# First output projection of a two-block layer in seven products instead of eight

## The chip, the cores and the metric

The kernel runs on one core of a Trainium2 chip. The metric is device time in microseconds; the kernel before takes 2780.12 us (median of 3 runs, 2779.41 to 2782.68). The engines are named as in the profile: PE (TensorE) multiplies, ACT (ScalarE) and DVE (VectorE) do the elementwise work, POOL (GpSimd) a little of it and some transfers, SP only issues transfers. Each engine runs its own list of instructions in order; they meet at semaphores alone.

## The reference, cut to what matters

Two blocks follow each other, both in float32, on 512 tokens with width 2048. What the change touches is the end of the first block:

```python
# first block: y_a, y_b are [512, 2048] each
y_a = _rmsnorm(y * silu(z_ssd), g_ssd)
y_b = _rmsnorm(u * sg * silu(z_mlp), g_mlp)
mix = concatenate([y_a, y_b], axis=-1) @ w_out     # [512, 4096] @ [4096, 2048]
x = x + gate * _rmsnorm(mix, g_post)
# second block begins with h = rms_norm(x, norm_gain) * (1 + scale) + shift
```

A row factor of the norm (one number for each token) comes out of the product, so the kernel multiplies by it when it takes results out of PSUM: `ra` for the first 2048 columns of the concatenation, `rb` for the second.

## The kernel before, in words

**Precision.** Every float32 matrix is split into a high part (a copy rounded to fp32r, made by ACT) and a low part (the rest, made by DVE), and a product is three matmuls: high by high, high by low, low by high. A weight unit is 128 partitions by 1024 numbers, 512 KB. SP loads it into one of three buffers `RAW`, ACT makes `WH`, DVE makes `WL` (four buffers each), PE uses both. ACT and DVE make units two ahead of PE (`make(u + 2)`), SP loads four ahead (`raw_load(u + 4)`); a buffer `RAW` is free when `hi` and `lo` of its unit are made, `WH` and `WL` when PE has `used` the unit.

**The projection** (`o_unit`, line 535, and the loop around it) has 64 units, 192 to 255 (`AT_OUT` is 192). A unit holds 2 tiles of 128 rows by 512 columns of `w_out`. For each of 4 token blocks `k` and both tiles it gives three matmuls of 128x512: 24 matmuls a unit, 1536 in all. The outer loops are `half` (which part of the concatenation) and `nb` (which 512 output columns); the four token blocks stand in four PSUM banks, and two sets of four banks alternate. The inputs come from `SY` in DRAM, in 32 loads by POOL (`y_load`); ACT and DVE scale and split each one (`turn_half`). Results of half 0 are scaled into `O` by ACT, those of half 1 are added by DVE. The last four units are used in the order of token blocks, so that one block of `O` after another is complete while PE goes on.

**The tail.** For each token block `k`: squares of its four column blocks (ACT, `jk`), their sum (DVE), a factor (POOL, `first_factor`), the product with the gain `gg` (DVE, `gain_out`), the new x in two halves (DVE, `make_x1`), its squares (ACT, `XR<-O`), a second factor (POOL, `second_factor`), the scaled rows (`XR`, ACT and DVE), and then PE transposes them (`turn_row`, L838). The first matmul of the second block (L437 after 1797 us) needs transposed tiles of all four token blocks.

**Work that lies beside it.** The last gates of the first block (16 in number) are spread over PE's list: `gate(g)` is a generator on each engine, stepped between units. For gate g, SP loads `vg`, `wsg` and `bsg`, DVE makes `wsr` from `wsg` (four small operations), PE multiplies (L755), DVE makes `sgt` and goes on to `GA`. Gate 14 follows PE's first unit of the projection, gate 15 its third. SP may load gate g+1 only when DVE has made `sgt` of gate g.

## Time and profile before

| what | value |
|---|---|
| median of the runs | 2780.12 us |
| profiled execution, span from first to last instruction | 2778.7 us |
| PE busy | 2740.8 us, 99% |
| DVE, ACT, POOL busy | 1471.3, 1061.1, 339.1 us |
| TensorE clock granted, mean over the span | 0.998 of full speed |
| first matmul of the projection / last one / first of the second block | 1432.72 / 1783.88 / 1797.25 us |

The profile gives the profiled execution's time as its span, 2778.7 us; the median of the runs is 1.4 us more, for what lies before the first and after the last instruction. Starts are counted from the span's start. A matmul of 128x512 is listed with some 0.39 us because neighbours overlap in the array; what counts is the distance of their starts. A line can be that of a helper: L1031 is every operation of ACT, L1650, L1654 and L1658 are helpers of DVE, L2501 is every load of SP. The tile names tell them apart.

### The profile page before, as it was taken

How to read it: one execution, taken by the hardware profiler on the slowest of the kernel's cores; microseconds unless marked ns; L12 is line 12 of the kernel's file. 1: busy time of each engine (PE TensorE's matmuls, PEld its weight loads, DVE VectorE, ACT ScalarE, POOL GpSimd, SP SyncE). 2: the span in 40 equal slices, each digit the busy share in tenths (PEclk: the TensorE clock that was granted, in tenths of full speed). 3: DMA queues.
4: the chain of work that ended last, by engine and by line, in shares of the span. 5: the costliest groups of instructions: out<-in, count | busy, mean ns of one | idle time of the engine just before them, and what ended most of it. 6: DMA issues, size and time to landing. Idle time of an engine off the chain costs nothing. (4 is left out here: it accounts for less than half of the span.)

```text
span 2778.7 us, 33018 instructions
## 1 busy us (share of the span) xinstructions
PE 2740.8 (99%) x13142; PEld 2231.2 (80%) x13142; DVE 1471.3 (53%) x1794; ACT 1061.1 (38%) x1420; POOL 339.1 (12%) x417
## 2 busy tenths in 40 slices
PE   6999999999999999999999999899999999999999
PEld 3688888888888888888888888788888888788787
DVE  2377767765565456766652332634445443533733
ACT  3332222334333333433332332535556553442611
POOL 2101000102233323331310000100000000000000
PEclk9999999999999999999999999999999999999999
DMA  9667766744545464555454433332222223223252
GB/s 399 254 234 260 274 233 251 278 159 154 179 146 169 156 185 151 160 169 175 150 190 180 134 113 99 119 102 83 84 83 89 78 83 103 87 91 99 102 179 91
DMA packets 162120, 439.34 MB, mean 158 GB/s; under 512 B 14768, under 2 KB 59824, under 8 KB 151728
## 3 DMA queue, kind: packets, MB, share of 16 engines
q1 hardware_dynamic: 122208, 303.08, 32.7%
q0 software_dynamic: 16944, 97.18, 9.9%
q10 hardware_dynamic: 22816, 36.97, 3.8%
q8 instruction: 105, 1.72, 0.3%
q14 instruction: 47, 0.39, 0.0%
HBM read 398.11 MB, written 39.06 MB: 157 GB/s over the span
## 5 line engine op out<-in xcount | busy, mean ns | idle before, releaser
L1650 DVE TENSOR_TENSOR WL<-RAW,WH 128x1024 fp32r<-128x1024 f32 (+1 forms) x424 | 519.0, 1232 | 744.9 <-ACT WH L1031 568.9
L437 PE MATMUL PB<-HH,WH 128*128 128x512 f32 x2048 | 818.6, 400 | 2.4 <-DVE WL L1650 2.4
L442 PE MATMUL PB<-HL,WH 128*128 128x512 f32 x2048 | 801.6, 391 | 0.0
L443 PE MATMUL PB<-HH,WL 128*128 128x512 f32 x2048 | 801.3, 391 | 0.0
L1031 ACT ACTIVATE WH<-RAW 128x1024 fp32r<-128x1024 f32 (+1 forms) x424 | 433.4, 1038 | 444.0 <-PE PB L549 252.6
L547 PE MATMUL PB<-WH,HH 128*128 128x512 f32 x1248 | 490.0, 393 | 1.6 <-ACT Kr L1031 0.8
L549 PE MATMUL PB<-WH,HL 128*128 128x512 f32 x1248 | 486.1, 390 | 0.0
L548 PE MATMUL PB<-WL,HH 128*128 128x512 f32 x1248 | 485.9, 389 | 0.0
L437 PEld LDWEIGHTS PB<-HH,WH 128*128 128x128 f32 x2048 | 385.0, 188 | 103.3 <-issue 22.6
L442 PEld LDWEIGHTS PB<-HL,WH 128*128 128x128 f32 x2048 | 385.6, 188 | 65.6 <-issue 3.1
L443 PEld LDWEIGHTS PB<-HH,WL 128*128 128x128 f32 x2048 | 385.0, 188 | 66.2
L547 PEld LDWEIGHTS PB<-WH,HH 128*128 128x128 f32 x1248 | 234.4, 188 | 51.5 <-issue 2.5
L549 PEld LDWEIGHTS PB<-WH,HL 128*128 128x128 f32 x1248 | 234.3, 188 | 49.3
L548 PEld LDWEIGHTS PB<-WL,HH 128*128 128x128 f32 x1248 | 234.4, 188 | 49.0 <-issue 1.0
L1658 DVE SCALAR_TENSOR_TENSOR AACC<-AU,small,AACC 128x2048 f32<-128x2048 f32 x60 | 140.9, 2349 | 68.1 <-DMA AU<-in_w_ada 68.0
L441 PE MATMUL PB<-CL,WH 128*128 128x256 f32 x384 | 108.3, 282 | 0.0
L440 PE MATMUL PB<-CH,WH 128*128 128x256 f32 x384 | 107.7, 281 | 0.0
L2409 POOL TENSOR_TENSOR xw<-xk,wk 128x256 f32<-128x256 f32 x80 | 75.1, 964 | 262.9 <-ACT xk L1031 161.9
L445 PE MATMUL PB<-CH,WL 128*128 128x256 f32 x384 | 106.8, 278 | 0.0
L1031 ACT ACT_TABLE_LOAD x77 | 98.8, 1283 | 6.3 <-DVE wk L1650 3.5
L1658 DVE SCALAR_TENSOR_TENSOR ca<-zp,par,ca 128x512 f32<-128x512 f32 x128 | 95.4, 746 | 7.9 <-ACT ca L1031 6.9
L1031 ACT ACTIVATE zp<-PB 128x512 f32<-128x512 f32 x32 | 18.9, 603 | 188.3 <-PE PB L445 171.4
(326 smaller groups left out, 2534.4 us busy)
## 6 DMA issues: line engine op xcount, KB each, us to landing
RAW<-in_w_in_t SPq DMA_DIRECT2D x312, 512.0 KB, 3.6
AU<-in_w_ada POOLq DMA_DIRECT2D x64, 1024.0 KB, 5.5
RAW<-in_w_out_t SPq DMA_DIRECT2D x96, 512.0 KB, 3.6
bcb<-R SPq DMA_DIRECT2D x64, 256.0 KB, 6.1
S<-so ACTq DMA_DIRECT2D x24, 384.0 KB, 2.5
ebc<-R SPq DMA_DIRECT2D x32, 256.0 KB, 6.0
SY<-evb ACTq DMA_DIRECT2D x32, 256.0 KB, 2.9
yin<-SY POOLq DMA_DIRECT2D x32, 256.0 KB, 4.0
```

The lines of the kernel that those rows point to most:

```text
L437: h.matmul(banks[j], lh, m.HH[:, t, :], start=st, stop=False)
L440: h.matmul(cb, lh, m.CH[:, t, :], start=st and j == 0, stop=False, skip_group_check=True)
L441: h.matmul(cb, lh, m.CL[:, t, :], start=False, stop=False, skip_group_check=True)
L442: h.matmul(banks[j], lh, m.HL[:, t, :], start=False, stop=False)
L443: ins = h.matmul(banks[j], ll, m.HH[:, t, :], start=False, stop=en)
L445: ins = h.matmul(cb, ll, m.CH[:, t, :], start=False, stop=en, skip_group_check=True)
L547: h.matmul(bank, xh, wh[:, tt, :], start=t == 0, stop=False)
L548: h.matmul(bank, xh, wl[:, tt, :], start=False, stop=False)
L549: ins = h.matmul(bank, xl, wh[:, tt, :], start=False, stop=t == 15)
L1031: return h.activation(o, a, f, **kw)
L1650: return h.tensor_tensor(o, a, b, op)
L1658: return h.scalar_tensor_tensor(out=o, in0=a, scalar=sc, in1=b, op0=op0, op1=op1)
```

## The change

The projection is done by a form of Strassen's multiplication. It runs in 8 groups `q`; the chunk `c = q // 2` is a fourth of the 4096 rows of `w_out`, and `n = q % 2` a half of the output columns. In a group a 2 by 2 block product (tokens in halves, rows in halves, columns in halves of 512) takes 7 products `ph` instead of 8, each of 2 weight units (`ab`) and 24 matmuls of 128x512. The number of units goes from 64 to 112.

- **Left side.** The chunk of y is loaded by SP (`load_y`) into `F`, scaled in place by ACT (`scale_tile`), POOL makes four sums (`sum_S`, 128x1024 each), and each of the 7 forms is split into `FH` (ACT) and `FL` (DVE). Forms are made once for two groups.
- **Right side.** SP loads B11, B21 and B22 of a group. The four sums E, F, H and G are made in the tile: POOL issues a DMA that adds a block of `w_out` to what the buffer holds (`accum_op=ADD`). E, F and G follow each other in one pair of buffers, each added when DVE has made `lo` of the one before; H is added to B22's pair. Each such step is two DMAs of 512 KB.
- **PSUM.** Three pairs of banks, X, Y and Z, in the order Y, X, Z, Z, Y, Y, Y. A product that stays in its pair adds to what is there, and PE waits until the bank's content has been taken out. Taking out is `evacuate`: in the first two groups mostly ACT, after that DVE alone, 14 operations a group.
- **Squares and gains.** ACT squares finished blocks of `O` in group 7; 12 of the 16 products with the gain `gg` go from DVE to POOL, the other four stay on DVE. Token blocks 0 and 1 have their last part in products 1 and 4 of group 7, blocks 2 and 3 in products 5 and 6, the last two. `XR` and `gg` are loaded by SP instead of POOL.

```diff
-UNITS_IN, UNITS_OUT, UNITS_IN2, UNITS_OUT2 = 192, 64, 128, 32
+UNITS_IN, UNITS_OUT, UNITS_IN2, UNITS_OUT2 = 192, 112, 128, 32
...
+def form_unit(q, ph, ab):
+
+    return AT_OUT + 14 * q + 2 * ph + ab
...
+def pair_of(q, ph):
+
+    return (q % 2, 3, q % 2, 2, q % 2, 2, q % 2)[ph]
...
+def out_source(q, row, col, ab):
+    c, n = divmod(q, 2)
+    return (2 * n + col) * 16 + 4 * c + 2 * row + ab
+
+
+def forms_due(q, ph):
+    c = q // 2
+    if q == 0:
+        return {0: [(0, 3)], 1: [(0, 4)], 3: [(0, 5)], 4: [(0, 6)]}.get(ph, [])
+    if q % 2:
+        return [(c + 1, f) for f in {1: [0], 2: [1], 4: [2], 6: [3]}.get(ph, [])] if c < 3 else []
+    return [(c, f) for f in {0: [4], 1: [5], 2: [6]}.get(ph, [])]
+
+
+def tiles_due(q, ph):
+    c = q // 2
+    if c < 3 and q % 2 == 0 and ph == 6:
+        return [(c + 1, i) for i in range(4)]
+    if c < 3 and q % 2 and ph == 0:
+        return [(c + 1, i) for i in range(4, 8)]
+    return []
...
+    X, Y, Z = ([ring.popleft() for j in range(2)] for ring in (main, main, hb))
+    m.bank.update({(nm, j): b[j] for nm, b in (("X", X), ("Y", Y), ("Z", Z)) for j in range(2)})
+
+    def bank_ready(q, ph, j):
+        if q == 0 and ph < 3:
+            reuse((Y, X, Z)[ph][j])
+        elif ph < 3:
+            P.wait_ge(*at("ev", q - 1, (6, 1, 3)[ph], j))
+        else:
+            P.wait_ge(*at("ev", q, (2, 0, 4, 5)[ph - 3], j))
+
+    def product(q, ph):
+        for j in range(2):
+            bank = PB[(Y, X, Z, Z, Y, Y, Y)[ph][j]]
+            bank_ready(q, ph, j)
+            P.wait_ge(*at("fl", q // 2, ph))
+            for ab in range(2):
+                n = form_unit(q, ph, ab)
+                split_ready(n)
+                wh = m.WH[n % 4].rearrange("p (t c) -> p t c", t=2)
+                wl = m.WL[n % 4].rearrange("p (t c) -> p t c", t=2)
+                for tt in range(2):
+                    p = 2 * ab + tt
+                    xh, xl = m.FH[ph][:, p, j * 128:(j + 1) * 128], m.FL[ph][:, p, j * 128:(j + 1) * 128]
+                    h.matmul(bank, xh, wh[:, tt, :], start=p == 0 and ph < 3, stop=False,
+                             skip_group_check=True)
+                    h.matmul(bank, xh, wl[:, tt, :], start=False, stop=False, skip_group_check=True)
+                    ins = h.matmul(bank, xl, wh[:, tt, :], start=False, stop=p == 3, skip_group_check=True)
+                if j:
+                    ins.then_inc(*put(s.unit, "used", n))
+                elif ab:
+                    ins.then_inc(*put(s.block, "half", q, ph))
+            if q == 0:
+                step(bg2)
+
+    for q in range(GROUPS):
+        for ph in range(7):
+            product(q, ph)
+            if q == 0 and ph == 5:
+                drain(bg2)
+                b, bank = take(hb, "gate sums")
+                P.wait_ge(*at("GA", 15))
+                column_sums(b, bank, m.GA, "gate sums")
+                drop(hb, b, ("rb sum",))
...
+    def form_high(c, f):
+        if f in (0, 1, 6):
+            A.wait_ge(*at("y scaled", c, 3 if f == 0 else 7))
+            A.wait_ge(*at("S", c, {2: 1, 4: 2, 5: 3, 3: 4}[f]))
...
+        if c:
+            A.wait_ge(*at(*form_free(c, f)))
+        else:
+            A.wait_ge(*at("ra sum"))
+            A.wait_ge(*at("YA", 7, 1))
+        A.then(act(m.FH[f], m.form[f], ACT.Copy), "fh", c, f)
...
+        if (q, ph) in ((0, 0), (0, 2), (0, 4), (0, 6), (1, 0), (1, 2), (1, 3), (1, 6)):
+            return
+        c, n = divmod(q, 2)
+        k = j if ph in (0, 1, 3, 4) else 2 + j
+        col = 1024 * n + (0 if ph in (0, 1, 6) else 512)
+        dst = add = m.O[:, k, col:col + 512]
+        V.wait_ge(*at(*out_done(q, ph, j)))
+        V.wait_ge(*at("ran" if c < 2 else "rbn"))
+        if (q, ph) == (0, 1):
+            add = m.t1[j]
+            V.wait_ge(*at("sg", 15))
+            V.wait_ge(*at("sgt", 15))
+            V.wait_ge(*at("ev", 0, 0, j))
+        elif (q, ph) == (0, 3):
+            add = m.t2[j]
+            V.wait_ge(*at("gate sums"))
+            V.wait_ge(*at("ev", 0, 4, j))
+        elif ph in (1, 4, 5):
+            V.wait_ge(*at("ev", q, (0, 3, 2)[(1, 4, 5).index(ph)], j))
+        else:
+            V.wait_ge(*at("ev", q - 2, {0: 1, 3: 3 if q == 2 else 4, 2: 5, 6: 6}[ph], j))
+        r = (m.ran, m.rbn) if ph in (4, 5) else (m.ra, m.rb)
+        V.then(STT(dst, bank("YXZZYYY"[ph], j), r[c // 2][:, k:k + 1], add, ALU.mult, ALU.add), "ev", q, ph, j)
...
+    def add_load(q, ph, before, row, col, ab, *key):
+        i = pair_of(q, ph)
+        G.wait_ge(*at("lo", form_unit(q, before, ab)))
+        h.dma_start(m.WP[i][ab], I["w_out_t"][out_source(q, row, col, ab)], accum_op=ALU.add) \
+            .then_inc(*land(s.wsum[2 * i + ab], *key, q, ab))
...
+    sum_S(0, 1)
+    sum_E(0)
+    for i in 2, 3, 4:
+        sum_S(0, i)
+    for q in range(GROUPS):
+        sum_F(q)
+        sum_H(q)
+        sum_G(q)
+        if q % 2 and q < 7:
+            for i in 1, 2, 3, 4:
+                sum_S(q // 2 + 1, i)
+        if q < 7:
+            sum_E(q + 1)
...
+    for k in range(4):
+        gain(k, 0)
+        gain(k, 1)
+    gain(0, 2)
+    gain(1, 2)
     first_factor(0)
+    first_factor(1)
+    gain(2, 3)
+    gain(3, 3)
+    first_factor(2)
     second_factor(0)
-    first_factor(1)
+    first_factor(3)
     second_factor(1)
-    first_factor(2)
-    first_factor(3)
     second_factor(2)
     second_factor(3)
...
+    def load_B21(q, ab):
+        if q:
+            Y.wait_ge(*at("lo", form_unit(q - 1, 1, ab)))
+        else:
+            Y.wait_ge(*(at("used", AT_OUT - 2) if ab else at("lo", AT_OUT - 1)))
+        out_load(q, 1, 1, 0, ab, "B21")
...
     drain(bg)
-    for u in range(AT_OUT, AT_IN2):
-        raw_load(u + 4)
-        step(bg2, 2)
+    load_B21(1, 0)
+    load_B21(1, 1)
+    drain(bg2)
```

SP's list around the loads for gates 14 and 15 (`vg`, `wsg`, `bsg`; `RAW` are weight buffers). Before:

```order
436 L2501 DMA RAW_53<-in_w_out_t 128x1024 [waits lo,hi]
437 L2501 DMA RAW_54<-in_w_out_t 128x1024 [waits lo,hi]
438 L2501 DMA vg<-VT 128x512 [waits VT2,dve_side,pe_side]
439 L2501 DMA wsg<-in_w_s_t 128x128
440 L2501 DMA bsg<-in_bs 128x128
441 L2501 DMA RAW_55<-in_w_out_t 128x1024 [waits lo,hi]
442 L2501 DMA RAW_53<-in_w_out_t 128x1024 [waits lo,hi]
443 L2501 DMA vg<-VT 128x512 [waits VT3,dve_side,pe_side]
```

The same place now (`hold` are further weight buffers; rows 443 and 444 are `load_B21(1, 0)` and `load_B21(1, 1)`):

```order
442 L2683 DMA hold_190<-in_w_out_t 128x1024
443 L2683 DMA RAW_55<-in_w_out_t 128x1024 [waits lo]
444 L2683 DMA hold_191<-in_w_out_t 128x1024 [waits lo]
445 L2683 DMA vg<-VT 128x512 [waits VT2,dve_side,pe_side]
446 L2683 DMA wsg<-in_w_s_t 128x128
447 L2683 DMA bsg<-in_bs 128x128
448 L2683 DMA vg<-VT 128x512 [waits VT3,dve_side,pe_side]
```

The load for gate 14 stood behind the weight load of unit 196, whose buffer is free after `lo` and `hi` of unit 193; it now stands behind two loads that wait for `lo` of units 194 and 195.

DVE's list at the same place now (`wsr` is gate 14's; `WL2_62` and `WL3_63` are the low parts of units 194 and 195, `FL3_177` that of a form, the last two those of the sum E):

```order
941 L1758 TENSOR_TENSOR WL2_62<-RAW2_55,WH2_58 128x1024 [waits unit,hi,wp6]
942 L1758 TENSOR_TENSOR WL3_63<-hold4_191,WH3_59 128x1024 [waits unit,hi,wp7]
943 L1762 TENSOR_SCALAR wsr_139<-wsg_137,small_66 128x128 [waits wsg]
944 L1762 TENSOR_SCALAR wsr_139<-wsg_137,small_66 128x128 x3
945 L1758 TENSOR_TENSOR FL3_177<-E0_185,FH3_176 128x1024 [waits act_side]
946 L1758 TENSOR_TENSOR WL0_60<-RAW0_53,WH0_56 128x1024 [waits unit,hi,wsum0]
947 L1758 TENSOR_TENSOR WL1_61<-RAW1_54,WH1_57 128x1024 [waits unit,hi,wsum1]
```

`wsr` stands behind the low part of unit 195, and the E sums behind `wsr`.

POOL's list at the end of the projection now; before, it held only the eight factors there (each a TENSOR_SCALAR and a TENSOR_TENSOR on `small`):

```order
439 L2574 DMA hold_189<-in_w_out_t 128x1024 [waits lo]
440 L2574 DMA hold_190<-in_w_out_t 128x1024 [waits lo]
441 L2569 TENSOR_TENSOR O<-O,gg 128x512 [waits act_side,gg]
442 L2569 TENSOR_TENSOR O<-O,gg 128x512 [waits act_side] x9
443 L2446 TENSOR_SCALAR small<-small 128x1 [waits dve_side]
444 L2443 TENSOR_TENSOR small<-small,cst 128x1 [waits pool_side]
445 L2446 TENSOR_SCALAR small<-small 128x1 [waits dve_side]
446 L2443 TENSOR_TENSOR small<-small,cst 128x1 [waits pool_side]
447 L2569 TENSOR_TENSOR O<-O,gg 128x512 [waits act_side] x2
```

Ten products with the gain now stand between the last adding DMA and the first factor.

## Rows read from the trace of the kernel before

**Rows 1.** The page's first part: busy time, share, instructions of each engine.
```profile
PE 2740.8 (99%) x13142; PEld 2231.2 (80%) x13142; DVE 1471.3 (53%) x1794; ACT 1061.1 (38%) x1420; POOL 339.1 (12%) x417
```

**Rows 2.** Busy time by window; last columns clock, DMA share, GB/s.
```profile
1640.00:1760.00 120.00, 120.00 (x531) 99.41 (x530) 42.64 (x46) 31.36 (x46) 0.00 (x0) 1.00 0.30 97
1780.00:1800.00 20.00, 11.95 (x52) 9.63 (x51) 16.04 (x26) 16.17 (x26) 6.88 (x10) 0.74 0.37 147
```

**Rows 3.** PE's timeline where the projection begins: start, us, instruction [idle before].
```profile
1432.72 0.39 PE L547 MATMUL PB<-WH,HH 128*128 128x512 f32 x1
...
1438.52 1.13 PE L755 MATMUL PB<-wsr,vg 128*128 128x128 f32 x8 [0.20 <-DVE wsr L1654]
```

**Rows 4.** PE's timeline at its end and after it.
```profile
1783.88 0.40 PE L829 MATMUL PB<-WH,HL 128*128 128x512 f32 x1
1792.69 0.90 PE L838 MATMUL PB<-cst,XR 128*128 128x128 f32 x3 [7.76 <-ACT XR L1031]
1793.78 3.83 PE L838 MATMUL PB<-cst,XR 128*128 128x128 f32 x15 [0.18 <-DVE XR L1654]
1797.25 0.78 PE L437 MATMUL PB<-HH,WH 128*128 128x512 f32 x1
```

**Rows 5.** Groups by line, 1640 to 1760: busy, mean ns, idle before.
```profile
L1650 DVE TENSOR_TENSOR WL<-RAW,WH 128x1024 fp32r<-128x1024 f32 x22 | 26.7, 1223 | 58.4 <-ACT WH L1031 58.4
L1031 ACT ACTIVATE WH<-RAW 128x1024 fp32r<-128x1024 f32 x22 | 22.9, 1056 | 63.2 <-PE PB L549 63.2
L1658 DVE SCALAR_TENSOR_TENSOR O<-PB,small,O 128x512 f32<-128x512 f32 x12 | 9.0, 750 | 18.6 <-PE PB L549 18.6
L1031 ACT ACTIVATE jk<-O 128x512 f32<-128x512 f32 x12 | 7.6, 632 | 25.1 <-DVE O L1658 25.1
L1031 ACT ACTIVATION_READ_ACCUMULATOR jk<-O 128x1 f32 x12 | 2.2, 187 | 0.0
```

**Rows 6.** SP's timeline about the gate loads.
```profile
1427.30 0.37 SPq L2501 DMA_DIRECT2D vg<-VT  x1
1436.34 3.57 SPq L2501 DMA_DIRECT2D RAW<-in_w_out_t  x2
1441.93 0.42 SPq L2501 DMA_DIRECT2D wsg<-in_w_s_t  x1
```

**Rows 7.** DVE's timeline about the last two gates.
```profile
1435.04 1.23 DVE L1650 TENSOR_TENSOR WL<-RAW,WH 128x1024 fp32r<-128x1024 f32 x1 [0.20 <-issue]
1437.51 0.86 DVE L1654 TENSOR_SCALAR wsr<-wsg,small 128x128 f32<-128x128 f32 x4
...
1447.71 0.88 DVE L1654 TENSOR_SCALAR wsr<-wsg,small 128x128 f32<-128x128 f32 x4 [0.86 <-DMA wsg<-in_w_s_t]
```

**Rows 8.** POOL's elementwise operations by tile and source: ns min/median/max.
```profile
L2436 POOL TENSOR_TENSOR YA<-YA,ysq x16: 1272/1294/1432, 733.8 to 1378.9; 128x512 f32<-128x512 f32 x16
L2425 POOL TENSOR_TENSOR htmp<-Sst,etot x64: 612/944/1627, 686.9 to 1338.3; 128x256 f32<-128x256 f32 x64
```

**Rows 9.** DVE's timeline while POOL is in such operations.
```profile
1329.51 1.80 DVE L1650 TENSOR_TENSOR WL<-RAW,WH 128x1024 fp32r<-128x1024 f32 x1 [2.07 <-ACT WH L1031]
```

**Rows 10.** DMA issues: queue, count, KB each, median us to landing.
```profile
RAW<-in_w_out_t SPq DMA_DIRECT2D x96, 512.0 KB, 3.6
RAW<-in_w_in_t POOLq DMA_DIRECT2D x8, 512.0 KB, 7.2
```

**Rows 11.** The page's second part: GB/s in 40 slices.
```profile
GB/s 399 254 234 260 274 233 251 278 159 154 179 146 169 156 185 151 160 169 175 150 190 180 134 113 99 119 102 83 84 83 89 78 83 103 87 91 99 102 179 91
```

**Rows 12.** Tile XR: ns min/median/max of its operations.
```profile
L1658 DVE SCALAR_TENSOR_TENSOR O<-O,small,XR x8: 1277/1284/1289, 1771.0 to 1789.1; 128x1024 f32<-128x1024 f32 x8
L1031 ACT ACTIVATE XR<-O x8: 1057/1058/1066, 1772.3 to 1790.4; 128x1024 f32<-128x1024 f32 x8
L1031 ACT ACTIVATE XR<-O,small x4: 1133/1143/1157, 1775.9 to 1793.2; 128x1024 f32<-128x1024 f32 x4
```

**Rows 13.** POOL's timeline: the last factor's second operation.
```profile
1792.65 0.54 POOL L2319 TENSOR_TENSOR small<-small,cst 128x1 f32<-128x1 f32 x1
```

More of the change, by code:

```diff
@@ L792, in tensor_program @@
     drain(bg)
-    for half in range(2):
-        for nb in range(4):
-            i = 4 * half + nb
-            banks = [4 * (i % 2) + k for k in range(4)]
-            def ready(t):
-                P.wait_ge(*at("yh", 16 * half + t))
-                P.wait_ge(*at("yl", 16 * half + t))
-            for kk in range(8 if i < 7 else 4):
-                o_unit(AT_OUT + 8 * i + kk, kk, banks, ready, i)
-                step(bg2, 2)
-                if i == 0 and kk == 6:
-                    b, bank = take(hb, "gate sums")
-                    P.wait_ge(*at("GA", 15))
-                    column_sums(b, bank, m.GA, "gate sums")
-                    drop(hb, b, ("rb sum",))
-            drain(bg2)
-            for k in range(4):
-                freed[4 * (i % 2) + k] = [("O", i, k)]
@@ L1306, in scalar_program @@
         make(96 + 8 * b + 9)
-        for L in ahead(96 + 8 * b + 7, AT_OUT):
-            turn_half(L)
         step(bg2)
@@ L2456, in gpsimd_program, with add @@
[L2456 to L2462 removed]
+    G.wait_ge(*at("ra"))
+    G.then(h.tensor_scalar(m.ran, m.ra, -1.0, None, ALU.mult), "ran")
+    def add(o, a, b, op, *key):
+        return G.then(h.tensor_tensor(o, a, b, op), *key)
+    def add_load(q, ph, before, row, col, ab, *key):
[3 more added lines that the diff above has]
+            .then_inc(*land(s.wsum[2 * i + ab], *key, q, ab))
@@ new lines, in gain @@
+    def gain(k, nb):
+        dst = m.O[:, k, 512 * nb:512 * nb + 512]
+        G.wait_ge(*at("gg"))
+        G.wait_ge(*at("O squared", nb, k))
+        add(dst, dst, m.gg[:, 512 * nb:512 * nb + 512], ALU.mult, "Og", nb, k)
+    sum_S(0, 1)
+    sum_E(0)
+    for i in 2, 3, 4:
+        sum_S(0, i)
+    for q in range(GROUPS):
+        sum_F(q)
[6 more added lines that the diff above has]
+            sum_E(q + 1)
+        if q == 1:
+            G.wait_ge(*at("rb sum"))
+            mean_power(m.rb, 2048, "rb")
+            G.wait_ge(*at("rb"))
+            G.then(h.tensor_scalar(m.rbn, m.rb, -1.0, None, ALU.mult), "rbn")
```

464 lines of the change are left out of this document (282 added, 182 removed).

## The prediction

> **What bounds the kernel now.** I read the page's first part, then busy time by window, then PE's timeline at both ends of the projection. PE is busy 99% of the span and DVE 53% [rows 1]: only fewer matmuls, or a shorter gap on PE, shorten the run. Inside the projection PE never idles; in 120 us of it DVE is busy 43 us, ACT 31, the clock is 1.00 and DMA moves 97 GB/s [rows 2]. The projection begins at 1432.72 [rows 3] and its last matmul starts at 1783.88 [rows 4]: 1536 matmuls of 128x512, with two gates (1.1 us each, as in [rows 3]) and the gate sums between. 351.4 us less some 3.2 for these is 0.2267 us a matmul. Behind it PE idles 7.76 us for scaled rows, runs its transposes on a lower clock (0.74 in that window), and the second block's first matmul comes at 1797.25, 13.1 us after the projection's end at 1784.1 [rows 2, 4]. The profile's time is its span, 2778.7 us; the median of the runs is 1.4 us more. I work on the span and add 1.4 at the end.
>
> **1. Matmuls.** 8 groups x 7 products x 24 are 1344 instead of 1536. 192 x 0.2267 = 43.5 us go, all of them on the path. A product takes 24 x 0.2267 = 5.44 us, a group 38.1.
>
> **2. DVE and ACT beside it.** From [rows 5]: a low part 1.22 us, taking out one bank 0.75, a high part 1.06. Per group from the third on DVE has 14 low parts (17.1), 14 banks (10.5) and 3 or 4 forms (at most 4.9): 32.5 of 38.1 us, hidden. ACT has 14 x 1.06 and at most 4 forms and 4 scalings, some 22 us. The order within a product matters as well, since two products in one bank pair need the bank taken out between. Let a product begin at T. DVE takes out the last bank of the product before (T+0.3 to 1.05), makes two low parts (to 3.5), takes out the first bank, full at T+2.7 (to 4.3), and may make a form (to 5.5). PE wants the first bank at T+5.44: 1.1 us to spare. Cost nothing. If that cover went, each microsecond of delay on DVE beyond 1.1 would be one on PE.
>
> **3. POOL's sums.** Four sums of 128x1024 for each of three later chunks. The trace has POOL at 1.29 us for 128x512 and 0.61 to 1.63 for 128x256 [rows 8]; bounds for 1024 columns are 2.5 and 6.5 us. DVE is slower too while POOL works: a low part took 1.80 us instead of 1.22 [rows 9]. With 4 us each they end 1.7 us after the last product of the odd group begins, where the last form may be late by some 5 us before PE feels it. DVE gets 6.5 us of work in products of 5.44 twice. I take 0.3 us for each of three odd groups, 1 us in all; bounds 0 and 12 (at 6.5 us a sum, some 4 us a group).
>
> **4. The adding DMAs.** No row has one. A weight sum is two of them, 512 KB each. Each is issued when the low part of its predecessor in the buffer is made, and ACT wants it two products later. DVE ends these low parts at T+2.3 and T+3.5, ACT wants them at T+10.9+0.3 and one high part later: 8.7 us without any delay, 9.8 with the 1.1 of step 2. A plain 512 KB took 3.6 us to land from SP and 7.2 from POOL in a stretch of heavy traffic [rows 10]. Bounds for an adding one are 3.6 and, at twice the slower, 14.4. I take 7, near the upper of the two rows, as two come together and SP loads beside them: hidden. At 14.4 each of three successive sums a group would be 4.6 late: 24 x 4.6 = 110 us. Traffic: a group loads 3 MB of weights and 1 MB of y plainly and adds 4 MB, in 38.1 us: 110 GB/s plain, 110 adding. If an added byte costs double, the sum is 330, against the 399 that the first slice of the page reached [rows 11].
> The Trainium skill (Collectives: The Full Stack, "The bandwidth ceiling: the fold count and why AG ≠ RS ≠ AR") says that a reduction in the DMA engines costs not because of the addition but because it reads two sources, half of a copy's rate. By it the sum would be the 330 GB/s above and nothing would be added; no row here shows it.
>
> **5. Gate 14.** Its load was issued at 1427.30 [rows 6]. Now it stands on SP behind two weight loads that wait for the low parts of units 194 and 195. The low part of 194 was made at 1435.04 to 1436.27 [rows 7]; ACT cannot make these high parts earlier, it first takes out the banks of PE's last unit before the projection. So 195's ends at 1437.5, `wsg` is issued at 1438.3. Gate 15's `wsg` was issued at 1441.93 and `wsr` began at 1447.71, DVE waiting for it [rows 6, 7]: 5.8 us. `wsr` then ends at 1438.3 + 5.8 + 0.9 = 1445.0, and PE wanted gate 14 at 1438.3 [rows 3]: 6.5 us of standstill, nothing beside it. What is queued behind `wsr` on DVE (a form, the two low parts of E) is made by 1448.7, before PE ends product 1. Gate 15 follows from gate 14 by about 7 us on SP and DVE and is wanted two products later, about even. I take 6.5; bounds 3 (landing in 2.3) and 11.
>
> **6. The tail.** Let E be the end of the last matmul. Before, ACT had to do after E: four squarings of x1 halves (1.06 + 0.19), one of O (0.63 + 0.19) and two scalings (1.14) [rows 5, 12], 8.1 us, and the second block began at E+13.1. Now blocks 2 and 3 end in the last two products, and ACT has seven squarings of x1, two of O, four scalings and two high parts: 8.8 + 1.6 + 4.6 + 2.1 = 17.1 us. That alone is 9 more. Besides, POOL's ten gain products stand ahead of the first factor. The last adding DMA waits for a low part made at E-18.3, so they start at E-17.2; at 1.37 us they end at E-3.5, at 1.8 (DVE beside them) at E+0.8. DVE needs the factor for x1 of block 0 (1.28 us a half [rows 12]) and stands until then with the last banks behind it. I walked the lists with 1.4 us: the last factor ends at E+20.6, where before it ended at 1793.2, 4.1 us ahead of L437 [rows 4, 13]. So L437 at E+24.7, or about E+28 with 1.8 us. I take E+26.5, 13.4 us later than before; bounds 9 and 18.
>
> **Sum.** -43.5 + 1 + 0 + 6.5 + 13.4 = -22.6. The span becomes 2756.1, the median 2757.5.
>
> **Rivals.**
> A. The adding DMAs are the bound, slower than before. One latency L, from the low part before to landing; beyond 9.8 us each of the 24 successive sums is late by L - 9.8. From L = 10.7 the gain is gone; at L = 12, 24 x 2.2 = 53 us: 2757.5 + 53 = 2810. For it: no such DMA in the trace, 7.2 us for a plain one under load, two at once. Against it: 3.6 us in this stretch [rows 10], a third of the bandwidth free.
> B. The traffic is the bound. If an added byte costs three times a plain one, a group moves 4.2 + 3 x 4.2 = 16.8 MB, at 399 GB/s [rows 11] in 42.1 us, 4 too long: 8 x 4 = 32 us, 2789.5. Nothing in the rows bears on the factor; the stretch before runs at a share of 0.30 for 97 GB/s [rows 2], so there is room.
> C. Gate 14 and the tail are covered: `wsg` comes early, ACT and DVE overlap better than my walk. Steps 5 and 6 cost 3 + 9: 2778.7 - 43.5 + 12 + 1.4 = 2748.6. For it: step 5 uses one wait. Against: the ACT count.
> D. The change doesn't save the matmuls because PE waits for banks in each group, 1 us for each of 31 products that follow another in their pair (four a group, but not the first): 2788.5. The order of step 2 speaks against it, with 1.1 us to spare.
>
> **How the numbers follow.** Forecast 0.50, A 0.20, B 0.07, C 0.18, D 0.05. What a measurement can tell from no change is 0.2%, 5.6 us: 2774.5 to 2785.7. Faster: the forecast and C, 0.68. Same: the mild ends of A, B and D, 0.07. Slower: the rest of these, 0.25. Range: below by C with a reserve, 2744; above into A up to 2802. The forecast's own range is 2750 to 2768.
>
> **What would show it.** Right: 1344 matmuls of 128x512 at 0.227 us with no pause from the second group on; one pause of about 6 us before the gate after the first product, ended by DVE's `wsr`; landings of adding DMAs below 9; L437 some 26 us after the last of them. Wrong: pauses of PE once a product ended by `WL` or by ACT's high part waiting for `wsum` (A, and with DMA share near 1, B); pauses ended by taking out (D); no pause at the gate (C). The lower clock after a long pause would add 1 to 3 us that I have counted only as far as before had it.

## The result and the profile after

The changed kernel takes 2797.48 us (median of 4 runs, 2795.98 to 2798.64) against 2781.3 for the kernel before on the same chip: ratio 1.0055, 95% interval 1.0040 to 1.0069. It is slower by half a per cent, where 0.8% less was forecast. The profiled execution has a span of 2794.2 us; the forecast for it was 2756.1, so 38.1 us have to be found.

The page's first part, of the kernel after: engine, busy time, share, instructions, as in [rows 1]. PE does 28.7 us less work, 192 matmuls fewer having promised 43.5, and its share fell from 99% to 97%.

```profile
PE 2712.1 (97%) x12950; PEld 2197.7 (79%) x12950; DVE 1613.9 (58%) x1906; ACT 1137.8 (41%) x1496; POOL 437.6 (16%) x474
```

PE's waits between 1420 and 1830 in the kernel after: what waited, for whom, us in total, times, longest. In the kernel before PE had no pause inside the projection.

```profile
PE PB L886 <- DVE O L1766: 22.3, 12, 8.4
PE PB L915 <- ACT XR L1107: 18.1, 3, 7.0
PE PB L822 <- DVE wsr L1762: 7.6, 1, 7.6
PE PB L886 <- ACT evb L1107: 0.7, 1, 0.7
```

The first line is what the forecast did not have (it put it at 1 us): twelve times PE waits for a bank that DVE has yet to take out (L1766 is DVE's helper for it). The projection's matmuls are L886, L888 and L889, a gate's L822, the transposes before the second block L915, that block's first matmul L504. PE's timeline of the kernel after, the longest pauses and the tail (start, us, instruction, idle before and what ended it; compare [rows 3, 4]):

```profile
1434.61 0.49 PE L886 MATMUL PB<-WH,FH 128*128 128x512 f32 x1 [0.69 <-ACT evb L1107]
...
1448.04 2.05 PE L822 MATMUL PB<-wsr,vg 128*128 128x128 f32 x8 [7.56 <-DVE wsr L1762]
...
1516.51 0.50 PE L886 MATMUL PB<-WH,FH 128*128 128x512 f32 x1 [2.13 <-DVE O L1766]
...
1732.16 0.80 PE L886 MATMUL PB<-WH,FH 128*128 128x512 f32 x1 [4.23 <-DVE O L1766]
...
1775.77 0.79 PE L886 MATMUL PB<-WH,FH 128*128 128x512 f32 x1 [8.45 <-DVE O L1766]
1776.36 0.63 PE L888 MATMUL PB<-WL,FH 128*128 128x512 f32 x1
1776.79 0.63 PE L889 MATMUL PB<-WH,FL 128*128 128x512 f32 x1
...
1801.50 1.33 PE L915 MATMUL PB<-cst,XR 128*128 128x128 f32 x5 [6.95 <-ACT XR L1107]
...
1812.99 0.78 PE L504 MATMUL PB<-HH,WH 128*128 128x512 f32 x1
```

Read the starts, not only the brackets. After a long pause the matmuls start 0.43 us apart instead of 0.23, up to nine of them: the clock is at its lower level (1.2 GHz) there. The windows of the kernel after, columns as in [rows 2], show it: 0.50 in the first 3 us behind the pause of 4.23 us, where [rows 2] had 1.00 inside the projection, and 0.88 over the last 84 us:

```profile
1475.00:1513.00 38.00, 38.00 (x170) 31.03 (x169) 24.25 (x25) 27.18 (x34) 10.95 (x10) 1.00 0.98 242
1732.20:1735.20 3.00, 3.00 (x7) 2.42 (x8) 2.83 (x3) 0.00 (x0) 0.86 (x1) 0.50 0.02 5
1716.00:1800.00 84.00, 60.60 (x245) 47.91 (x243) 56.54 (x56) 35.48 (x60) 30.94 (x33) 0.88 0.58 152
```

The first of these lines has a second finding, in the last columns: a group without any pause, and the DMA engines busy 0.98 of the time for 242 GB/s. From 1475 to 1680 us the share is 0.88.

**Where the 38.1 us are**, from PE's timeline against the forecast's terms:

- Waits for banks in the projection: 22.3 us, forecast 1. +21.3.
- Lower clock: 44 starts come more than 0.3 us behind that of a matmul of the projection, with no pause between, 28 of them at the lower clock (0.43 us or a little more). Together they take 8.0 us more than at 0.2267. Forecast 0. +8.0.
- Restarts: around the 13 pauses PE loses more than the idle time in the brackets, 2.1 us in all. Forecast 0. +2.1.
- Pace: most of the time three matmuls take 0.70 us and not 0.68. 313 such triples of the records cost 5.7 us together: +5.7.
- The gate: 7.56 for 6.5. +1.1.
- The projection begins at 1434.61, not 1432.72. +1.9, of which 0.7 is the wait for `evb` above. In the profiled executions of the runs below it begins anywhere from 1432.6 to 1437.9, so the rest may be chance.
- The tail: the last matmul ends at 1788.8, L504 starts at 1812.99, 24.2 us later. Forecast 26.5. -2.3.

That is 37.8 of 38.1. Past L504 both kernels need the same: 981.2 and 981.5 us.

**The longest pause.** DVE's timeline and POOL's in the kernel after, about 1762 (start, us):

```profile
1762.43 12.62 DVE L1758 TENSOR_TENSOR WL<-hold,WH 128x1024 fp32r<-128x1024 f32 x2
1774.97 1.40 DVE L1766 SCALAR_TENSOR_TENSOR O<-PB,small,O 128x512 f32<-128x512 f32 x2
```
```profile
1760.15 12.68 POOL L2569 TENSOR_TENSOR O<-O,gg 128x512 f32<-128x512 f32 x10
```

Two low parts, 1.2 us each elsewhere, take 12.62 us together. The first takes 11.49 of them and ends at 1773.92, 1.1 us behind the last of POOL's ten gain products (1772.83): it does its own work only when they are over. POOL's run at 1.27 us each, undisturbed. Taking out the next banks, which PE waits for, stands behind them on DVE. The same at smaller size in the odd groups, when POOL makes its sums; DVE's timeline there (1.2 us each would be normal for every low part, `WL` or `FL`):

```profile
1510.54 5.25 DVE L1758 TENSOR_TENSOR WL<-hold,WH 128x1024 fp32r<-128x1024 f32 x2 [3.12 <-ACT WH L1107]
1515.71 0.74 DVE L1766 SCALAR_TENSOR_TENSOR O<-PB,small,O 128x512 f32<-128x512 f32 x1
1516.37 2.73 DVE L1758 TENSOR_TENSOR FL<-E,FH 128x1024 fp32r<-128x1024 f32 x1
```

**The adding DMAs.** In the kernel after all 64 landed within 5.5 to 14.2 us of their issue, median 6.9:

```profile
L2574 POOL DMA_DIRECT2D hold<-in_w_out_t x40: 854/863/1216, 1458.0 to 1759.6; - x40
L2574 POOL DMA_DIRECT2D RAW<-in_w_out_t x24: 863/867/1218, 1423.7 to 1714.8; - x24
...
DMA to landing us min/median/max: 5.5/6.9/14.2
```

The median is the 7 us that was assumed. The maximum is not inside the window of 9.8: nine of the 64 took longer than 9.8. The last two of group 6, issued at 1714.3 and 1714.8, were awaited by ACT until 1724.1 and 1729.1, and they are what led to the pause of 4.23 us. ACT's timeline:

```profile
1724.14 1.06 ACT L1107 ACTIVATE WH<-RAW 128x1024 fp32r<-128x1024 f32 x1 [4.39 <-DMA RAW<-in_w_out_t]
1729.06 1.06 ACT L1107 ACTIVATE WH<-RAW 128x1024 fp32r<-128x1024 f32 x1 [3.85 <-DMA RAW<-in_w_out_t]
```

The last two of group 7, issued at 1758.4 and 1759.6, landed after 10.9 and 13.6 us, beside the last load of x and the first weights of the second block (issued from 1756.3 on). They fall into the longest pause, so that it has two causes at once; run 1 parts them.

### The profile page after: what moved, and what is told of

Read it like the earlier page. It is cut to its first block and busy times, and to the rows that moved or that the text cites. A ratio compares the mean times of both kernels' runs of the same rounds, so it can differ in the third digit from the quotient of the medians.

```text
span 2794.2 us, 32956 instructions
## 1 busy us (share of the span) xinstructions
PE 2712.1 (97%) x12950; PEld 2197.7 (79%) x12950; DVE 1613.9 (58%) x1906; ACT 1137.8 (41%) x1496; POOL 437.6 (16%) x474
## 5 line engine op out<-in xcount | busy, mean ns | idle before, releaser
L504 PE MATMUL PB<-HH,WH 128*128 128x512 f32 x2048 | 818.0, 399 | 3.1 <-DVE WL L1758 3.1
L504 PEld LDWEIGHTS PB<-HH,WH 128*128 128x128 f32 x2048 | 384.9, 188 | 104.2 <-issue 22.9
L614 PE MATMUL PB<-WH,HH 128*128 128x512 f32 x768 | 303.0, 395 | 1.6 <-ACT Kr L1107 0.8
L616 PE MATMUL PB<-WH,HL 128*128 128x512 f32 x768 | 299.4, 390 | 0.0
L615 PE MATMUL PB<-WL,HH 128*128 128x512 f32 x768 | 299.2, 390 | 0.0
L886 PE MATMUL PB<-WH,FH 128*128 128x512 f32 x448 | 180.2, 402 | 22.9 <-DVE O L1766 22.3
L1766 DVE SCALAR_TENSOR_TENSOR AACC<-AU,small,AACC 128x2048 f32<-128x2048 f32 x60 | 141.2, 2353 | 74.1 <-DMA AU<-in_w_ada 73.9
L888 PE MATMUL PB<-WL,FH 128*128 128x512 f32 x448 | 179.4, 400 | 0.0
L889 PE MATMUL PB<-WH,FL 128*128 128x512 f32 x448 | 177.5, 396 | 0.0
L614 PEld LDWEIGHTS PB<-WH,HH 128*128 128x128 f32 x768 | 144.2, 188 | 33.1 <-issue 2.5
L615 PEld LDWEIGHTS PB<-WL,HH 128*128 128x128 f32 x768 | 144.3, 188 | 30.3 <-issue 1.0
L616 PEld LDWEIGHTS PB<-WH,HL 128*128 128x128 f32 x768 | 144.2, 188 | 30.4
L886 PEld LDWEIGHTS PB<-WH,FH 128*128 128x128 f32 x448 | 85.7, 191 | 48.7 <-DVE O L1766 27.4
L1758 DVE TENSOR_TENSOR WL<-hold,WH 128x1024 fp32r<-128x1024 f32 x72 | 108.9, 1544 | 13.1 <-ACT WH L1107 11.9
```

What stands on the lines that cost most here:

```text
L504: h.matmul(banks[j], lh, m.HH[:, t, :], start=st, stop=False)
L614: h.matmul(bank, xh, wh[:, tt, :], start=t == 0, stop=False)
L615: h.matmul(bank, xh, wl[:, tt, :], start=False, stop=False)
L616: ins = h.matmul(bank, xl, wh[:, tt, :], start=False, stop=t == 15)
L886: h.matmul(bank, xh, wh[:, tt, :], start=p == 0 and ph < 3, stop=False, skip_group_check=True)
L888: h.matmul(bank, xh, wl[:, tt, :], start=False, stop=False, skip_group_check=True)
```

## The experiments

Runs 1 to 8 are the changed kernel with the edit shown, run 9 is run 8 with one more edit, run 10 is run 9 with one more. "Less" is meant against 2797.5, with 1 to 2 us of uncertainty. The kernel before took 2781.3 us beside the changed kernel and 1.2 to 1.5 us less beside the runs, so that much of each "less" need not come from the edit. The last column of the table, from the profiled execution of each, is free of that: the time from the projection's first matmul to the second block's first.

| run | median, us | kernel before beside it, us | first matmul to L504 (before: L437), us |
|---|---|---|---|
| kernel before | | | 364.5 |
| changed kernel | 2797.48 | 2781.30 | 378.4 |
| 1 wait between gains | 2793.28 | 2780.13 | 375.6 |
| 2 forms exchanged | 2795.59 | 2780.13 | 378.1 |
| 3 forms in the lower area | 2794.27 | 2780.09 | 376.2 |
| 4 gates' loads first | 2792.67 | 2780.13 | 376.0 |
| 5 x behind the weights | 2790.28 | 2780.13 | 373.7 |
| 6 sums on DVE | 2785.13 | 2780.09 | 367.1 |
| 7 plain loads | 2786.75 | 2780.09 | 369.2 |
| 8 together | 2762.37 | 2780.09 | 345.8 |
| 9 fewer y loads beside | 2761.36 | 2779.77 | 344.7 |
| 10 tail reordered | 2762.06 | 2779.77 | 343.9 |

### 1. A wait between the gain products

```diff
+        if gained:
+            G.wait_ge(*at(*gained[-1]))
         add(dst, dst, m.gg[:, 512 * nb:512 * nb + 512], ALU.mult, "Og", nb, k)
+        gained.append(("Og", nb, k))
```

> Each gain product on POOL waits for the gain product before it; nothing else is changed. In the changed kernel ten of them ran back to back from 1760.15 to 1772.83, one low part on DVE took 11.49 us inside that stretch, and PE stood 8.45 us until DVE took out a bank. Theory 1 (POOL keeps DVE's low parts, which read two tensors from SBUF, away for as long as POOL's instructions follow each other without a wait, and DVE gets in where POOL waits for its own result): low parts there last at most 4 us, the pause of PE shrinks from 8.45 us to under 3, and the time falls by 6 to 9 us, to about 2790. Theory 2 (only the sum of POOL's work counts, whatever stands between the instructions): the pause stays at 8 us or more and the time at 2797.5. Theory 3 (the late adding DMAs, landed 13 us after their issue, hold the stretch): the pause stays as well, since the DMAs are not touched.

Measured: 2793.28, 4.2 less where 6 to 9 were expected. POOL's and DVE's timelines in this run:

```profile
1759.24 17.92 POOL L2569 TENSOR_TENSOR O<-O,gg 128x512 f32<-128x512 f32 x10
```
```profile
1761.53 1.85 DVE L1758 TENSOR_TENSOR WL<-hold,WH 128x1024 fp32r<-128x1024 f32 x1
1764.37 1.25 DVE L1758 TENSOR_TENSOR WL<-hold,WH 128x1024 fp32r<-128x1024 f32 x1 [0.99 <-ACT WH L1107]
...
1768.77 1.97 DVE L1758 TENSOR_TENSOR WL<-hold,WH 128x1024 fp32r<-128x1024 f32 x1 [1.56 <-ACT WH L1107]
1772.61 1.76 DVE L1758 TENSOR_TENSOR WL<-hold,WH 128x1024 fp32r<-128x1024 f32 x1 [1.88 <-ACT WH L1107]
```

The low part of 11.49 us is gone, none is over 2. So what kept DVE away was the unbroken row of POOL instructions: where POOL waits for its own result, DVE gets a turn. Theory 1 holds for the mechanism. The pause shrank only from 8.45 to 4.67, against the under 3 that was expected, because a second cause lay below the first: ACT's high parts at 1767.6 and 1771.45 wait for adding DMAs issued at 1757.55 and 1758.68, 10 and nearly 13 us before. They were as late in the changed kernel, where the row of POOL instructions hid them. Theory 3 was half right. Each cause is enough for a pause: with the row broken up 4.67 us stay, and without the late DMAs (run 7) 8.19.

### 2. Two forms change places in SBUF

```diff
-    for i, off in enumerate((WA, WA + 40 * KB, WA + 32 * KB, 0, WA + 48 * KB, 8 * KB, 16 * KB)):
+    for i, off in enumerate((WA, WA + 40 * KB, WA + 32 * KB, WA + 48 * KB, 0, 8 * KB, 16 * KB)):
```

> The forms of products 3 and 4 change places in SBUF (form 3 goes to the upper area where forms 0, 1, 2 and 4 lie, form 4 to the lower area where 3, 5 and 6 lie); nothing else. In the changed kernel the matmuls of products 0, 1, 2 and 4 start 0.2333 us apart and those of 6 and of the second halves of 3 and 5 start 0.2267 us apart; before the change all did. Theory 1 (the place of the stationary tile in SBUF sets the pace): product 3 is now slow in both halves, product 4 is the fast one in its second half or in both, and the total stays at 2797.5 within 2 us. Theory 2 (the pace hangs on the place of the product in the group, its banks or what the other engines do beside it): the pattern of slow and fast stays with the numbers of the products.

Measured: 2795.59. PE's timeline in the second half of product 4 of group 4, first the kernel after, then this run:

```profile
1636.58 0.39 PE L886 MATMUL PB<-WH,FH 128*128 128x512 f32 x1
...
1637.28 0.39 PE L886 MATMUL PB<-WH,FH 128*128 128x512 f32 x1
```
```profile
1635.66 0.39 PE L886 MATMUL PB<-WH,FH 128*128 128x512 f32 x1
...
1636.34 0.39 PE L886 MATMUL PB<-WH,FH 128*128 128x512 f32 x1
```

L886 to L886: 0.70 and 0.68 us. In groups without pauses the slow run of triples went from 28 (products 0, 1, 2 and the first half of 3) to 36 (up to the first half of 4), and the fast one moved behind it. The pace goes with the place of the stationary tile: theory 1. Its first half behind a slow product is slow too, in either layout; I have no cause for that.

### 3. All forms in the lower area

```diff
-    for i, off in enumerate((WA, WA + 40 * KB, WA + 32 * KB, 0, WA + 48 * KB, 8 * KB, 16 * KB)):
+    for i, off in enumerate((32 * KB, 40 * KB, 24 * KB, 0, 48 * KB, 8 * KB, 16 * KB)):
...
-    hold = [at(f"hold{i}", (32 + 4 * i) * KB, [128, 1024]) for i in range(5)]
+    hold = [at(f"hold{i}", WA + k * KB, [128, 1024]) for i, k in enumerate((0, 4, 40, 44, 48))]
```

> All seven forms (the stationary tiles of the products) lie in the lower area of SBUF, in the first 56 KB; the weight buffers that PE does not read lie in the upper one instead. The first form of product 2 is made one product later, all else is as in the changed kernel (2797.5). Exchanging forms 3 and 4 moved the slow pace of 0.2333 us with the place, so by theory 1 (the place of the stationary tile) all matmuls of the projection now run 0.2267 us apart outside the stretches of low clock, which is 1344 x 0.77 x 0.0067 = 7 us less: about 2790.5. Theory 2 (only the change from one area to the other, or the first half behind it, is slow): less than 2 us. The pauses that DVE ends stay: they have 5.44 instead of 5.6 us a product now, so they may grow by up to 0.3 us each, 3 us in all.

Measured: 2794.27, 3.2 less by the medians, 2.2 by the last column. In the groups' undisturbed stretches the triples are at 0.68, and what the slower ones cost fell from 5.7 us to 0.4. But PE's pauses in the projection, the gate's included, grew from 29.8 to 33.8 us (the longest from 8.45 to 9.11): it arrives sooner at banks that are no readier. 5.3 us less work and 4.0 more waiting leave little. Where an engine waits for another, a faster one wins little.

### 4. The gates' loads first on SP

```diff
+    drain(bg2)
     load_B21(1, 0)
     load_B21(1, 1)
-    drain(bg2)
```

> The loads of gates 14 and 15 stand on SP ahead of the two weight loads of product 1 of the second group. Theory 1 (step 5 of the prediction: the gate's load stands behind two loads that wait for low parts): the pause of 7.56 us before gate 14 goes or falls under 1 us, the slow clock behind it goes with it (9 matmuls of 0.43 instead of 0.23, 1.8 us), and the time falls by 7 to 9 us, to about 2789. Theory 2 (DVE is late at that point anyway, a form's low part took 5.99 us there and two products of gates 3.5, so the scaling of the gate would be made after 1440 all the same): the pause falls only to 3 to 5 us and the time by 3 to 5.

Measured: 2792.67, 4.8 less by the medians (its four executions lie 6.6 us apart), 2.4 by the last column. PE stands 2.07 us before gate 14 and 1.29 before gate 15, for 7.56 and nothing. DVE's timeline before gate 14 in this run shows what is left:

```profile
1429.14 5.99 DVE L1758 TENSOR_TENSOR FL<-E,FH 128x1024 fp32r<-128x1024 f32 x1
...
1435.66 3.49 DVE L1758 TENSOR_TENSOR evb<-evb,ub 128x512 f32<-128x512 f32 x2
...
1440.64 1.22 DVE L1758 TENSOR_TENSOR WL<-hold,WH 128x1024 fp32r<-128x1024 f32 x1
1441.78 0.87 DVE L1762 TENSOR_SCALAR wsr<-wsg,small 128x128 f32<-128x128 f32 x4
```

The weights are there, and DVE reaches the scaling (`wsr`) only at 1441.78, since POOL's first sums held its form and `evb` up (5.99 for 1.2 us, 3.49 for 1.3). Both theories had a part: the queue on SP some 4 of the 7.56 us (2.07 and 1.29 are left). That POOL has the rest is read from the lengths, not tried by itself; it fits run 8, where with the sums on DVE as well gate 14's wait is 0.84 us.

### 5. The loads of x behind the weights

```diff
+        load_B22(q + 1, 0)
+        load_B22(q + 1, 1)
         if q == 6:
             Y.wait_ge(*at("fl", 3, 6))
             for k in range(3):
                 load(m.XR[:, k, :], I["x"][0, k * 128:(k + 1) * 128, :], s.xr[k], "XR", k)
-        load_B22(q + 1, 0)
-        load_B22(q + 1, 1)
```

> The three loads of x (1 MB each) are issued behind the two weight loads of product 3 of the last group, not ahead of them. Theory 1 (these 3 MB delay the weight loads, which landed at 1724 and 1729; ACT and DVE then made the weights late and PE stood 4.23 us): the pause at 1728 goes, with the slow clock behind it, and the time falls by 5 to 6 us, to about 2792. Theory 2 (the queue is full in any order, at the DMA share of 1.03 in that stretch, and another transfer is late instead): the pause moves or comes back elsewhere in the last two groups and the time falls by less than 2 us.

Measured: 2790.28, 7.2 less by the medians, 4.7 by the last column; the pause of 4.23 us is gone, and none came in its place in the last two groups. Small ones elsewhere grew by 2.3 us in all (0.68 to 1.62 in group 1, 0.66 before gate 15). Theory 1 in effect, though it named the wrong transfer: ACT had waited for the last adding DMAs of group 6 (`RAW`, issued at 1714.3 and 1714.8 on POOL's queue), beside the 3 MB of x, issued from 1710.64. Now x is issued from 1720.63, and the two DMAs landed after 5.7 and 7.6 us instead of 9.8 and 14.2.

### 6. The sums of forms on DVE

```diff
-        if q % 2 and q < 7:
-            for i in 1, 2, 3, 4:
-                sum_S(q // 2 + 1, i)
...
+            if q % 2 == 0 and ph == 0:
+                sum_S(q // 2, 3)
+            if q % 2 and q < 7 and ph in (1, 3, 5):
+                sum_S(q // 2 + 1, (1, 2, 4)[ph // 2])
```

> The 16 sums of forms (128x1024) are made on DVE, one in each of four products of a group, not on POOL; all else is as in the changed kernel (2797.5). On DVE one costs 1.22 us like a low part. Theory 1 (POOL's sums keep DVE's low parts away: 2.7 to 4.1 us each instead of 1.2, and this makes the pauses 2.13 + 0.68, twice 0.7 + 0.3 + 1.7): these eight pauses go, with 2 us of low clock behind the first, 8 to 10 us in all: about 2788.5. Theory 2 (DVE simply has too much to do in the odd groups): DVE gets 4.9 us more work in each, the pauses stay or grow, and the time is 2797 or more. The pauses of 0.64 and 0.73 us in groups 2 and 4 are left in either case.

Measured: 2785.13, 12.3 less by the medians, 11.3 by the last column, more than theory 1 said. DVE's timeline at the place shown above:

```profile
1510.56 2.36 DVE L1758 TENSOR_TENSOR WL<-hold,WH 128x1024 fp32r<-128x1024 f32 x2 [1.99 <-ACT WH L1107]
1512.84 0.74 DVE L1766 SCALAR_TENSOR_TENSOR O<-PB,small,O 128x512 f32<-128x512 f32 x1
1513.50 1.21 DVE L1758 TENSOR_TENSOR FL<-E,FH 128x1024 fp32r<-128x1024 f32 x1
```

DVE got 16 more instructions and PE's pauses in the odd groups vanished. The gates' and those of 0.96, 0.90, 4.26 and 8.46 us stayed. With 3.7 us more in an odd group and 1.2 in an even one DVE keeps up (busy 162 of the 205 us from 1475 to 1680); with POOL beside it, it had not. Theory 2 is out.

### 7. Plain loads for the adding ones

```diff
-        h.dma_start(m.WP[i][ab], I["w_out_t"][out_source(q, row, col, ab)], accum_op=ALU.add) \
+        h.dma_start(m.WP[i][ab], I["w_out_t"][out_source(q, row, col, ab)]) \
```

> The 64 adding DMAs load plainly over their buffer: the sums of weights are left out, the number of transfers, their bytes and their order stay. Theory 1 (step 4 of the prediction: the added transfers are hidden, since their 7 us lie in a window of 9.8): the landings become shorter, the DMA share falls from 0.95 to about 0.6, and the time stays within 2 us of 2797.5, since the pauses come from POOL's gains, the sums, the gate and the loads of x. Theory 2 (their cost in the DMA engines, double that of a plain byte or more, makes the loads of product 3 and the last sums late): the pause of 4.23 us goes and the time falls by 5 to 8 us.

Measured: 2786.75, 10.7 less: theory 2, and more of it. DMA queues, packets, MB and share of the 16 engines, between 1475 and 1680, first in the kernel after, then in this run (q0 carries POOL's transfers):

```profile
q0 software_dynamic: 5760, 20.97, 56.1%
q1 hardware_dynamic: 10988, 22.54, 31.6%
...
F<-SY SPq DMA_DIRECT2D x23, 256.0 KB, 11.3
```
```profile
q1 hardware_dynamic: 11136, 23.07, 33.3%
q0 software_dynamic: 5760, 20.97, 29.9%
...
F<-SY SPq DMA_DIRECT2D x23, 256.0 KB, 6.8
```

The same 5760 packets cost 1.88 times as much when they add, while the other queue's cost hardly changed. The median landing went from 6.9 to 4.6 us, that of a y tile, which adds nothing, from 11.3 to 6.8. The pauses of the even groups went, and 4.23 became 0.92; the gate (7.37) and the gains (8.19) stayed. DVE's low part beside the ten gain products still took 11.22 us, so it is not the adding DMAs that held it.

### 8. All edits together

Edits 3 to 6, eight of the gain products on DVE, and the last load of x and the second block's first weights held back by two products (the last two were not tried by themselves):

```diff
+            if q == 7 and 1 <= ph <= 4:
+                gain(ph - 1, 0)
+                gain(ph - 1, 1)
...
-            Y.wait_ge(*at("used", form_unit(7, 2, 1)))
+            Y.wait_ge(*at("used", form_unit(7, 4, 1)))
             load(m.XR[:, 3, :], I["x"][0, 384:512, :], s.xr[3], "XR", 3)
```

> All together: forms in the lower area, sums of forms and eight of the twelve gain products on DVE, the gates' loads and the weight loads of product 3 ahead, the last load of x and the first of the second block's weights held back until product 4 of the last group is done. The parts by themselves: pace -7, sums -9, gate -5, loads of x -7 (all measured or expected beside the changed kernel), gains -10. If they add up, 2797.5 - 38 = 2759.5, faster than the kernel before by 0.7%. If DVE becomes the bound with 4.9 us of sums more in each odd group and products of 5.44 us, pauses of 1 to 2 us come back in three groups: 2765 to 2770. If the adding DMAs are too late once PE waits for nothing else, pauses ended by ACT's high part appear in every group and the time stays above 2780.

Measured: 2762.37 (2760.97 to 2764.93), ratio to the kernel before 0.9941, 95% interval 0.9924 to 0.9957. The change gains 0.6% once what it disturbed is put right; of the 38 us expected if the parts add up, 35.1 came. PE's waits between 1420 and 1800:

```profile
PE PB L915 <- ACT XR L1107: 19.2, 3, 7.0
PE PB L822 <- DVE wsr L1762: 5.4, 2, 4.6
PE PB L886 <- DVE O L1766: 2.9, 2, 1.6
...
```

22.3 us for banks have become 2.9. From the first matmul of the projection to L504 it needs 345.8 us; the changed kernel needed 378.4, the kernel before 364.5. Gate 15's wait (4.58) is now the longest in the projection.

### 9. Fewer y loads beside the adding DMAs

```diff
...
+        if q % 2 == 0 and q < 6:
+            Y.wait_ge(*at("used", form_unit(q, 4, 1)))
+            load_y(q // 2 + 1, range(4, 8))
...
-            Y.wait_ge(*at("sgt", g - 1))
...
         load(m.wsg, I["w_s_t"][g], s.wsg, "wsg", g)
+        if g:
+            Y.wait_ge(*at("sgt", g - 1))
```

> The combined kernel (2762.4, span 2759.2) with two loads moved: the second four of the eight y tiles of a chunk are loaded after product 4 of the even group, behind the weight loads of product 3, and gate 15's weights no longer wait for gate 14's row of biases to be used. In the combined kernel the y loads (1537.1 to 1549.6) ran beside the last adding DMAs of an even group, which landed 10 and 11 us after their issue (at 1549.1 and 1551.7), and PE stood 1.64 and 1.26 us in groups 2 and 4; before gate 15 it stood 4.58 us. Theory 1 (an adding DMA is late only where another large load falls beside it): landings there fall under 9 us, both pauses go, and gate 15's falls under 1.5: 2.9 + 3 + 1.5 of low clock, about 2755. Theory 2 (adding DMAs are that slow by themselves): the pauses in groups 2 and 4 stay, and only the gate's 3 to 4.5 us are won: 2758.5.

Measured: 2761.36, not to be told from run 8. Gate 15's wait halved (4.58 to 2.23), the two pauses became 1.85 and 1.96, and behind the first of these seven matmuls ran at the lower clock. ACT's timeline in this run:

```profile
1548.53 1.06 ACT L1107 ACTIVATE WH<-RAW 128x1024 fp32r<-128x1024 f32 x1 [3.04 <-DMA RAW<-in_w_out_t]
1552.18 1.06 ACT L1107 ACTIVATE WH<-RAW 128x1024 fp32r<-128x1024 f32 x1 [2.58 <-DMA RAW<-in_w_out_t]
```

They were issued at 1539.37 and 1540.75: 9.2 and 11.4 us. Half of the y loads (1537.35 to 1541.6) still lie at their start and the weights of the next group (1544.5) beside them, so this run does not part theory 1 from 2. Whether an empty queue would bring them under 9 us stays open.

### 10. Another order of the tail

```diff
     square_out(2, 2)
-    scale_x1(0)
     square_x1(1, 0)
     square_out(3, 2)
+    scale_x1(0)
...
+    second_factor(0)
     first_factor(2)
-    second_factor(0)
     first_factor(3)
```

> As the run before it, and the tail in another order: ACT squares x1 and O of the next blocks before it scales block 0, and POOL makes block 0's second factor before block 2's first. In the combined kernel ACT idled 4.38 us for that factor, 1753.9 to 1758.3. Theory 1 (the tail hangs on this factor and on ACT's list behind it): the first scaled row comes 1.6 us earlier and the second block's first matmul 3 to 4 us, 2751.5. Theory 2 (the tail hangs on the sum of ACT's work behind the last product): 1 us or less is won. By the prediction's step 6 ACT has 17.1 us of work behind the end and L504 came 24 us behind it, so 7 us are waits, and part of them can go.

Measured: 2762.06, nothing won in the time against run 9. In the trace the tail did get shorter: L504 comes 22.9 us behind the end of the last matmul, 25.3 in runs 8 and 9. ACT's wait for block 0's factor fell from 4.38 to 1.90 us, of PE's three waits before the transposes the second shrank from 6.95 to 4.89 and the others hardly changed, and the first scaled row came 0.3 us earlier, not 1.6. So 2.3 us were won in the tail, between the two theories, and by the waits they come from the later blocks more than from block 0; that was not tried by itself. Inside the projection this execution lost 1.6 us again, by five further pauses of 0.3 to 0.8 us. Two of them, at 1508 and 1514, lie long before the first changed instruction, so the edit did not make those; the cause of the others is open.

## Why the prediction was wrong

The forecast had the gate and the tail about right and the number of matmuls right. It went wrong where it had put a cost at nothing or next to nothing: the waits for banks (steps 2 and 3, and the gains of step 6), 22.3 us for 1; the lower clock and the restarts behind them, 10.1 for 0; and the pace (step 1), 5.7 for 0.

- **Step 1, matmuls.** 192 went, but 0.2267 us holds for a stationary tile where the kernel before had it. With four of the seven forms in the upper area, and the half product behind them slow as well, the pace is 0.2333 most of the time: 5.7 us, shown by run 2 (the slow pace moves with the form) and run 3 (5.3 us of it go). The change's lines on addresses stood in the diff, and I gave them no cost.
- **Steps 2 and 3, DVE and POOL.** This is the step that failed most. I took a low part of 1.80 us beside POOL [rows 9] as a rate, a DVE somewhat slower as long as POOL works. It is a turn to be waited for: in a row of ten POOL instructions DVE's next one waits for the end of all. I put POOL's sums at +1 us; moving them to DVE gave 11.3 (run 6, last column). That is within my upper bound of 12, but by luck: the bound stood for slow sums of 6.5 us, and POOL was even quicker than the 4 us that I took, 2.4 to 3.4 us a sum. The Trainium skill (SBUF — State Buffer, "Who interferes with whom") says that a DVE instruction with two SBUF inputs contends with a GpSimd one that reads SBUF, and in the section "SBUF: two separate sides" that whichever of the two starts first has the shared ports for the whole instruction. The trace agrees: the low part of 11.49 us has two inputs in SBUF, while taking out a bank, with only one of its two large tensors in SBUF, kept its 0.74 us at 1515.71 while a sum of POOL was under way. Run 1 adds that the hold reaches over instructions that follow each other without a wait. Step 2's spare 1.1 us a product could not carry that.
- **Step 6, the gains.** The ten products began at E-28.7; without the pause that they caused and its low clock that is some 10 us nearer to E, where E-17.2 was said. I asked only when the first factor would be ready, not what stood beside them on DVE: 8.45 us of pause inside the projection and nine starts at the lower clock, some 2 us. Not all of it is the gains' alone, since with their row broken up 4.67 us of pause stay for the late adding DMAs of step 4 (run 1). The tail itself was right: the last factor ended at E+20.1 (walked: 20.6), L504 came at E+24.2 (24.7 by the same walk, 26.5 taken).
- **Step 4, the adding DMAs.** Landing 7 us in the median, as assumed; factor 1.88 for an adding byte, near the 2 assumed, as the Trainium skill has it (Collectives: The Full Stack, the section named in step 4: half of a copy's rate). But I divided 330 by 399 GB/s from the page's first slice, and at the plain transfers' own cost here (20.97 MB in 29.9% of 205 us) the engines would reach, as an estimate, 342 GB/s when all busy. They were 0.98 busy in the window shown, and where other large loads (x, y, weights) lay beside them nine landings took 10 to 14 us, beyond the window of 9.8. Plain loads instead are worth 9.2 us (run 7, last column; 10.7 by the medians): not "hidden, 0". For the loads of x run 5 shows it; that an adding DMA without any neighbour always lands in time was not shown (run 9). It is a small part of rival A and of B, at a few places instead of in every group.
- **Step 5, gate 14.** 7.56 us for 6.5, by the queue on SP as said (some 4 us back in run 4). The size is partly luck: the low parts began at 1439.0 and 1440.2, not at 1435.0 and 1436.3, with POOL's first sums beside DVE, but from the issue of `wsg` to `wsr` it took 4.8 us and not 5.8, and PE itself came 2.2 us later than assumed.
- **The lower clock after a pause** was named at the end with 1 to 3 us. With four pauses over 2 us, and a slower start after each of the others, it is 8.0, and 2.1 for the restarts.

Run 8 comes within 5 us of the forecast of 2757.5, but by taking away what step 3, step 4 and the gains had cost; it doesn't make the forecast right. Of the rivals D was the nearest in kind, PE waiting for banks, but for a reason that it did not have. Its sign, pauses ended by taking out, is the one that came. The chance of 0.25 for slower was too low, because the waits of steps 2 to 4, the pace and the clock were put at or near nothing, where each could only grow.

## What to carry to other kernels

Before work goes to POOL, list DVE's instructions with two SBUF inputs beside it, and count each as blocked for the whole unbroken row of POOL instructions; break such rows up with waits, or give the work to DVE even where it is much used already (busy 165 of 205 us of the projection in run 8). A DMA that adds costs almost two plain ones; check the engines' busy share, not the GB/s, before you call it hidden. And a term set to nothing because of spare time should carry the sum of all that uses the same spare time.
